# The expert stage's gather: one product for a pair of groups, in place of one for each group

## The reference, cut to what matters

```
scores = sigmoid(h @ w_router)             # 16 experts in 4 groups of 4
best   = argmax over groups of the sum of the two best biased scores
gate   = the two best experts of that group, weights normalised
a = h @ w_gate[e]; u = h @ w_up[e]         # 2048 -> 512
act = silu(a) * u * gate[e]
y  += act @ w_down[e]                      # 512 -> 2048
```

## Time and profile before

| | |
|---|---|
| median of three runs | 2128.92 us |
| span of the profiled execution, first to last instruction | 2125.9 us |
| the same execution around the span, by the median | 3.0 us |
| TensorE busy | 2011.4 us, 95% of the span, 10876 matmuls |
| VectorE busy | 1491.2 us, 70% |
| ScalarE busy | 951.2 us, 45% |
| first gather begins, first weight tile of group 0 | 1459.9 us, 1474.2 us |
| stretch 1474.2 to 2095 us: TensorE, VectorE, ScalarE busy | 610.7, 542.4, 436.4 of 620.8 us |
| bytes moved in that stretch | 318 GB/s |

### The profile page before, as it was taken

How to read it: one execution, slowest core, us unless ns; L and a number is a source line. 1 busy time by engine, 2 the same in 40 slices (tenths; PEclk the granted TensorE clock), 3 DMA queues, 4 the chain that set the end, 5 groups by cost and what they waited for, 6 DMA issues and landing times. The chain is left out here.

```text
span 2125.9 us, 27975 instructions
## 1 busy us (share of the span) xinstructions
PE 2011.4 (95%) x10876; PEld 1744.8 (82%) x10876; DVE 1491.2 (70%) x2174; ACT 951.2 (45%) x1360; POOL 7.8 (0%) x12
## 2 busy tenths in 40 slices
PE   8799999989999999999999969997999999999995
PEld 2299988977888999999999958876777887787774
DVE  0467675548877777765777733355889889889996
ACT  1333565331454322223322233343767667667773
POOL 0000000000000000000000000000000000000000
PEclk9999999999999999999999989997999999999997
DMA  9934333333433555563455566532999989899992
GB/s 374 395 123 142 118 129 110 121 125 135 158 127 134 187 208 198 200 232 118 162 209 203 199 205 230 211 123 80 330 311 357 312 312 340 307 319 338 350 348 95
DMA packets 133513, 460.96 MB, mean 217 GB/s; under 512 B 17568, under 2 KB 23520, under 8 KB 133248
## 3 DMA queue, kind: packets, MB, share of 16 engines
q1 hardware_dynamic: 133376, 459.12, 61.0%
HBM read 455.06 MB, written 4.00 MB: 216 GB/s over the span
## 5 line engine op out<-in xcount | busy, mean ns | idle before, releaser
L185 DVE TENSOR_TENSOR wlo<-raw,whi 128x1024 fp32r<-128x1024 f32 x640 | 779.4, 1223 | 426.6 <-ACT whi L179 407.1
L179 ACT ACTIVATE whi<-raw 128x1024 fp32r<-128x1024 f32 x640 | 678.8, 1061 | 839.2 <-PE bank L207 586.2
L205 PE MATMUL bank<-hhi,whi 128*128 128x384 f32 x1664 | 570.4, 343 | 9.2 <-DVE wlo L185 4.1
L206 PE MATMUL bank<-hlo,whi 128*128 128x384 f32 x1664 | 559.7, 336 | 0.0
L207 PE MATMUL bank<-hhi,wlo 128*128 128x384 f32 x1664 | 559.6, 336 | 0.0
L205 PEld LDWEIGHTS bank<-hhi,whi 128*128 128x128 f32 x1664 | 315.0, 189 | 39.5 <-issue 25.1
L206 PEld LDWEIGHTS bank<-hlo,whi 128*128 128x128 f32 x1664 | 315.1, 189 | 0.8
L207 PEld LDWEIGHTS bank<-hhi,wlo 128*128 128x128 f32 x1664 | 314.9, 189 | 0.0
L257 DVE SCALAR_TENSOR_TENSOR cond_parts<-raw,cond_padded,cond_parts 128x512 f32<-128x512 f32 x360 | 250.6, 745 | 1.3 <-DVE rstd L71 0.2
L2170 PE MATMUL bank<-whi,group_hi 128*128 128x512 f32 x512 | 204.0, 398 | 7.1 <-DVE wlo L185 5.7
L2172 PE MATMUL bank<-wlo,group_hi 128*128 128x512 f32 x512 | 201.2, 393 | 0.0
(11 more groups left out here) (323 smaller groups left out, 2015.2 us busy)
## 6 DMA issues: line engine op xcount, KB each, us to landing
raw<-in_dense SPq DMA_DIRECT2D x448, 512.0 KB, 4.5
raw<-in_moe SPq DMA_DIRECT2D x384, 512.0 KB, 5.1
merged<-in_x SPq DMA_DIRECT2D x8, 768.0 KB, 7.2
cs_rows_bc<-cs_rows SPq DMA_DIRECT2D x8, 768.0 KB, 5.0
out_y<-y_normed SPq DMA_DIRECT2D x3, 768.0 KB, 4.9
shift_rows<-cs_rows SPq DMA_DIRECT2D x2, 1024.0 KB, 11.3
pool_w_sb<-in_pool_w SPq DMA_DIRECT2D x1, 1024.0 KB, 6.9
pool_inv_count<-in_pool_inv SPq DMA_DIRECT2D x1, 768.0 KB, 4.9
```

The source lines that it names most:

```text
L179: self.nc.scalar.activation(self.whi[:, k % W, :], self.raw[:, n % R, :], ACT.Copy).then_inc(self.hi_done, 1)
L185: self.nc.vector.tensor_tensor(self.wlo[:, k % W, :], self.raw[:, n % R, :], self.whi[:, k % W, :].bitcast(F32), ALU.subtract).then_inc(se ...
L205: self.nc.tensor.matmul(out, self.whi[:, s, c], xhi[:, k, :], start=(k == 0), stop=False)
L206: self.nc.tensor.matmul(out, self.whi[:, s, c], xlo[:, k, :], start=False, stop=False)
```

## The change

The matmuls of `pick_block` keep their 256 columns, but take the matrices of both groups of a pair, 2i and 2i+1, and both halves of the result are kept. Group 0's gather ahead of the stage now brings group 1 too. In the stage there is one gather, in group 1 (i + half = 1 with half = 1), for groups 2 and 3; groups 0 and 2 have none. Since xhi and xlo now hold a pair (the same memory in all), they can be overwritten only when group 1 has done its last up tile, t=79, so PICKS has new places, t=80 to 95, in banks that gate and up have left for good. The evictions are a whole bank, 128 x 512, one per pair p, and one tile earlier than the listed number. The wait of the first tile is finer: each of the eight gate tiles u waits for the low halves it reads, but the first for all of those that lie in its bank 0 (four; ahead of group 0, seven), and up0 for all eight. The zero slots with their memset and semaphore are gone, and the tiles behind them lie elsewhere in memory. Otherwise the order of all tiles, scatters and activations is the same.

```diff
-PICKS = [(1, (24, 25), 26), (0, (27, 28), 29), (0, (31, 33), 34), (0, (36, 37), 38),
-         (1, (48, 49), 50), (7, (51, 52), 53), (7, (55, 57), 58), (7, (60, 61), 62)]
+PICKS = [(0, (80, 81), 82), (7, (83, 84), 85), (1, (85, 86), 87), (0, (87, 88), 89),
+         (7, (89, 90), 91), (1, (91, 92), 93), (7, (93, 94), 95), (1, (95, 95), 96)]
 PICK_AFTER = [max([0] + [q + 1 for q in range(p) if PICKS[q][0] == PICKS[p][0]]) for p in range(8)]
+PICK_BANK0 = max(p + 1 for p in range(8) if PICKS[p][0] == 0)
...
         pick_at = N.at
-        self.pick = sb("pick", [P, NCH, NG + 2, P], F32R)
-        place_at = N.at
+        self.pick = sb("pick", [P, NCH, NG, P], F32R)
+        place_at = N.at = pick_at + KB * (P + NE) * 4
         self.place = sb("place", [P, NG + 1, T], F32R)
...
         at = N.at = after
-        self.xhi, self.xlo = [None, None], [None, None]
-        for h in range(2):
-            self.xhi[h], self.xlo[h] = sb(f"group_hi{h}", [P, KB, P], F32R), sb(f"group_lo{h}", [P, KB, P], F32R)
+        self.xhi, self.xlo = sb("pair_hi", [P, KB, 2, P], F32R), sb("pair_lo", [P, KB, 2, P], F32R)
         self.th = sb("ff_tanh", [P, 512], F32)
...
         names = ("picked", "place_tr", "place", "weights", "weights_sb", "steps", "gathered", "group_hi", "group_lo", "tanh",
-                 "silu", "act", "act_tr", "act_hi", "act_lo", "y_hi", "y_lo", "scattered", "x_added", "gate_now", "zero",
+                 "silu", "act", "act_tr", "act_hi", "act_lo", "y_hi", "y_lo", "scattered", "x_added", "gate_now",
                  "squares", "sums", "y", "y_stored", "diagonal", "root")
...
          self.s_si, self.s_act, self.s_at, self.s_ah, self.s_al, self.s_yh, self.s_yl, self.s_sc, self.s_x,
-         self.s_gc, self.s_zero, self.s_sq, self.s_sum, self.s_y, self.s_out, self.s_diag, self.s_root) = [sem("ff_" + n) for n in names]
+         self.s_gc, self.s_sq, self.s_sum, self.s_y, self.s_out, self.s_diag, self.s_root) = [sem("ff_" + n) for n in names]
...
-    def picked(g0, i, half):
-
-        return (i * 2 + (g0 + half + 1)) * 8
+    def paired(r, i):
+
+        return (2 * r + i) * 8
+
+    def pair(x, p):
+
+        return x[:, 2 * p:2 * p + 2, :, :].rearrange("p a h s -> p (a h s)")
...
-        @block.gpsimd
-        def _(pool):
-            nc.gpsimd.memset(E.pick[:, :, NG:NG + 2, :].bitcast(F32), 0.0).then_inc(E.s_zero, 1)
-
         @block.scalar
...
                 N.tile0 = first + 2 * body * r
-                def group_high(n, p, bank, x):
+                def pair_high(n, p, bank):
                     act.wait_ge(E.s_ga, n + (p + 1))
-                    A(x[:, 2 * p:2 * p + 2, :], B[bank][:, :].rearrange("p (a b) -> p a b", a=2)[:, :, 0:P], ACT.Copy)\
-                        .then_inc(E.s_gh, 1)
+                    A(pair(E.xhi, p), B[bank][:, :], ACT.Copy).then_inc(E.s_gh, 1)
...
                         for p, (bank, _tiles, at) in enumerate(PICKS):
-                            if t == at and i * 2 + half < NG - 1:
-                                group_high(picked(g0, i, half), p, bank, E.xhi[1 - half])
+                            if t == at - 1 and i * 2 + half == 1:
+                                pair_high(paired(r, 1), p, bank)
                 for g in range(NG):
...
                 for p in range(8):
-                    group_high(g0 * 8, p, p % 2, E.xhi[0])
+                    pair_high(paired(r, 0), p, p % 2)
                 for i in range(0, 2):
...
-                def group_low(n, p, bank, x, xh):
+                def pair_low(n, p, bank):
                     dve.wait_ge(E.s_gh, n + (p + 1))
-                    V.tensor_tensor(x[:, 2 * p:2 * p + 2, :], B[bank][:, :].rearrange("p (a b) -> p a b", a=2)[:, :, 0:P],
-                                    xh[:, 2 * p:2 * p + 2, :].bitcast(F32), ALU.subtract).then_inc(E.s_gl, 1)
+                    V.tensor_tensor(pair(E.xlo, p), B[bank][:, :], pair(E.xhi, p).bitcast(F32), ALU.subtract).then_inc(E.s_gl, 1)
...
                         for p, (bank, _tiles, at) in enumerate(PICKS):
-                            if t == at and i * 2 + half < NG - 1:
-                                group_low(picked(g0, i, half), p, bank, E.xlo[1 - half], E.xhi[1 - half])
+                            if t == at - 1 and i * 2 + half == 1:
+                                pair_low(paired(r, 1), p, bank)
                 if r:
...
                 for p in range(8):
-                    group_low(g0 * 8, p, p % 2, E.xlo[0], E.xhi[0])
+                    pair_low(paired(r, 0), p, p % 2)
                 if r == 0:
...
                 N.tile0 = first + 2 * body * r
-                def pick_block(g, k, bank, bl):
+                def pick_block(i, k, bank, bl):
...
                         tok = slice(c * P, (c + 1) * P)
-                        rhs = E.pick[:, c, ds(g, 2), :].rearrange("p a s -> p (a s)")
+                        rhs = E.pick[:, c, 2 * i:2 * i + 2, :].rearrange("p a s -> p (a s)")
                         nc.tensor.matmul(o, N.hhi[:, k, tok], rhs, start=(c == 0), stop=False)
...
                 def of_group(half):
-                    return lambda k: (E.xhi[half][:, k, :], E.xlo[half][:, k, :])
+                    return lambda k: (E.xhi[:, k, half, :], E.xlo[:, k, half, :])
...
                 def group(i, half):
-                    pe.wait_ge(E.s_gl, picked(g0, i, half))
                     for t, (kind, j, u) in enumerate(FF_ORDER):
...
                         for p, (bank, tiles, _at) in enumerate(PICKS):
-                            if i * 2 + half == NG - 1:
+                            if i * 2 + half != 1:
                                 break
-                            if t == tiles[0]:
-                                pe.wait_ge(E.s_gl, picked(g0, i, half) + PICK_AFTER[p])
-                            if t in tiles:
-                                last = pick_block(i * 2 + (half + 1), 2 * p + tiles.index(t), bank, tiles.index(t))
+                            if t == tiles[0] and bank == 0 and not PICK_AFTER[p]:
+                                pe.wait_ge(E.s_act, (g0 + half) * 4 + 2 + 2)
+                            elif t == tiles[0] and not PICK_AFTER[p]:
+                                pe.wait_ge(E.s_act, (g0 + half) * 4 + 3 + 2)
+                            elif t == tiles[0]:
+                                pe.wait_ge(E.s_gl, paired(r, 1) + PICK_AFTER[p])
+                            for bl in range(2):
+                                if t == tiles[bl]:
+                                    last = pick_block(1, 2 * p + bl, bank, bl)
                             if t == tiles[1]:
                                 last.then_inc(E.s_ga, 1)
-                        if u == 0 and j > 0 and kind != "down" and i * 2 + half < NG - 1:
-                            pe.wait_ge(E.s_gl, picked(g0, i, half) + sum(at < t for _b, _t, at in PICKS))
+                        if kind == "gate" and j == 0 and half == 0:
+                            pe.wait_ge(E.s_gl, paired(r, i) + max(u + 1, PICK_BANK0 if i else 7))
+                        if kind == "up" and j == 0 and u == 0 and half == 0:
+                            pe.wait_ge(E.s_gl, paired(r, i) + 8)
                         if kind == "gate":
...
                 pe.wait_ge(E.s_pl, g0 + NG)
-                pe.wait_ge(E.s_zero, 1)
                 for p in range(8):
                     if p >= 2:
-                        pe.wait_ge(E.s_gl, g0 * 8 + p - 1)
+                        pe.wait_ge(E.s_gl, paired(r, 0) + p - 1)
                     for bl in range(2):
```

## The result

The changed kernel takes 2100.53 us in the median of four executions (2097.09 to 2104.36), against 2129.28 us for the kernel before on the same chip: ratio 0.9864, 95% interval 0.985 to 0.9878. Measured a second time, beside the experiments, it took 2100.26 us, ratio 0.9868 (0.9851 to 0.9884). It is 1.3 to 1.4% faster. The forecast was 2103.9 us with a range down to 2101; the time lies 0.5 us under that range.

A forecast was written before the change was run, and what follows sets the result against it. TensorE was taken to bound the expert stage, VectorE close behind. Terms -12.2 - 12.2 - 1.1 + 0 + 0.5 = -25.0 us took the span from 2125.9 to 2100.9 us; 3.0 us around it gave 2103.9, range 2101 to 2110.

The forecast's parts named there:

- group 0: Expert stage, group 0: its gather of the next group removed, -12.2 us, with the loads' +0.5 us counted apart.
- group 2: Expert stage, group 2: its gather removed, leaving the same work as group 3 there, -12.2 us.
- group 1: Expert stage, group 1: gather moved from t=24 to 62 to t=80 to 95, -1.1 us in sum.
- first gather: Ahead of group 0: wider evictions cost time, the finer first-tile wait saves it; sum 0, bounds -0.6 and +1.5 us.
- local stall at t=83: Group 1: the gather's first block into bank 7 waits for the activation of j=3, 0.3 us late.
- The loads' margin: Group 0's weight loads: 0.8 us between the time available and the landing, nearly used up; cost +0.5 us.
- the loads didn't bind: Rival: transfers from memory limit group 0, giving 2106 to 2110 us; chance 0.12.
- the packed gather didn't stall: Rival: evictions and hand-overs stall TensorE in group 1, first gather at its upper bound, 2106 to 2111 us; chance 0.09.
- the time wasn't hidden: Rival: TensorE isn't the bound, its removed 22 us become idle time, 2127 us; chance 0.03.
- the serial chain: Rival: in group 1's t=80 to 95 TensorE sits out each pair's whole round, 28 us, 2132 us; chance 0.03.
- group 1's t=84 to group 2's t=20 longer by about 11 us: Sign expected in the changed profile: this stretch grows by about 11 us, where group 1's gather now stands.
- group 3 unchanged within 0.3 us: Sign expected in the changed profile: group 3, which gathers nothing, keeps its time within 0.3 us.

The follow-up runs named there:

- dead2: Changed kernel with 96 gather matmuls put back into group 2, results unread and no evictions; median 2113.15 us.
- onebank: Changed kernel with seven of the eight pairs of group 1's gather in bank 1; median 2110.80 us.
- again: The changed kernel unedited, run again for a second profile; median 2100.26 us, ratio 0.9868 to the kernel before.
- before_again: The kernel before, unedited, one execution for a second profile; groups 0 to 2 took 150.51, 157.21 and 157.09 us.
- silu_early: Changed kernel with the first activation instruction on VectorE moved to three tiles behind each gate product's end; median 2092.60 us, ratio 0.9835.
- ring5: Changed kernel with five raw buffers in place of six in the whole program; median 2154.66 us.
- two_of_three: Changed kernel without the third matmul of each expert weight tile, output incomplete; one execution, span 38 us shorter.
- undo2: Changed kernel with group 2's whole old gather put back: matmuls, evictions into spare tiles and waits; median 2112.12 us.
- narrow_first: Changed kernel with the first gather's evictions 256 columns wide again, output wrong; one execution, first gather matmul to first weight tile 13.49 us.
- lastwait: Changed kernel with the first two scatters of group 3's own output at t=94 in place of t=93; median 2100.54 us.
- both2: Changed kernel with the early first activation instruction and every group's scatters of t=89 and 92 at t=88 and 90; 2095.27 us, ratio 0.9853.
- before_silu: The kernel before with only the first activation instruction moved early; 2119.63 us, ratio 0.9964.

## Why the prediction was right and wrong

Right is the mechanism, step by step, by the means of two profiles: group 0 -11.6 us (forecast -12.2, +0.5 for the loads); group 2 -12.3 (-12.2); group 1 -1.3 (-1.1); first gather -0.3 (0). The sum of these steps is -25.5 us against -25.0. Between the transposes of t=20 and t=68 the groups took 69.9 and 69.3 us (forecast 69.4), 70.8 and 70.7 (70.5), 70.3 and 70.5 (70.6). The local stall at t=83 and the lost stall at t=84 came as described. The loads' margin was used as feared, but it cost little: ScalarE waited for transfers 2.7 us in group 0, and TensorE's matmuls for low splits 1.9 us there, 0.3 more than before. None of the rivals came: the loads didn't bind, the packed gather didn't stall, the time wasn't hidden (dead2), and the serial chain, which onebank comes nearest to, costs 8.8 us when it is forced.

One sign I had worked out wrong: "group 1's t=84 to group 2's t=20 longer by about 11 us". It is longer by 8.3 us (49.5 before, 57.9 after; 49.7 and 57.8 in the second profiles). The prediction put all sixteen blocks of the gather behind the transposes of t=84. Three of them and the wait of 0.38 us lie ahead, so from t=68 to there it is 2.5 us longer (25.0 before, 27.5 after). Together they are the 11 us.

Wrong is the forecast time and with it the place of the range, in three terms outside these steps.

First, "the median of the timed runs is 2128.9, 3.0 us more than the span, which I keep". The profiled execution was not the median one. What lies around a span is 2.0 us before (in each of the eleven executions beside again 1.9 to 2.1) and 1.8 after (the changed kernel's profiled execution: 2101.34 us, span 2099.6); the rest of the 3.0 was the distance to another execution. That is 1.0 to 1.2 us too much in the forecast. To keep it meant to take the steps off 2128.9, a median of three; the later medians of the kernel before, of 9 to 12 executions, are 2126.9 to 2127.7.

Second, "group 3 unchanged within 0.3 us". It came 1.5 us shorter by the means, and this term stood at nothing in the sum. In the order of time, the profile of before shows why. TensorE, ahead of the last tiles, after its wait of 1.80 us:

```profile
2083.07 0.63 PE L2170 MATMUL bank<-whi,ff_act_hi 128*128 128x512 f32 x1
2083.50 0.63 PE L2171 MATMUL bank<-whi,ff_act_lo 128*128 128x512 f32 x1
2083.93 0.63 PE L2172 MATMUL bank<-wlo,ff_act_hi 128*128 128x512 f32 x1
```

and after the change, after a wait of 1.85 us at the same place:

```profile
2058.19 0.39 PE L2167 MATMUL bank<-whi,ff_act_hi 128*128 128x512 f32 x1
2058.42 0.40 PE L2168 MATMUL bank<-whi,ff_act_lo 128*128 128x512 f32 x1
```

The pitch is 0.43 us in the one and 0.23 in the other: the granted clock is 0.50 for that stretch of before, 1.2 GHz, and 1.00, 2.4 GHz, in the changed kernel. I had read these rows as tail and not compared their pitch. From the matmul behind the wait to the first of the last tile, the same 20 matmuls take 5.80 us in the one and 4.22 in the other, and that is nearly all of group 3's difference:

```profile
2082.02:2087.82 5.80, 5.80 (x20) 4.99 (x21) 3.72 (x8) 1.42 (x3) 0.00 (x0) 0.71 0.00 0
2057.42:2061.64 4.22, 4.22 (x20) 3.72 (x21) 3.72 (x8) 1.42 (x3) 0.00 (x0) 1.00 0.01 2
```

(5.84 in before_again, 4.22 in again.) It doesn't follow the gathers: dead2, silu_early, ring5 and two_of_three have the slow stretch too, the last three with the changed kernel's gathers as they are; again, undo2, onebank, narrow_first, lastwait and both2 don't; both profiles of before and that of before_silu do.

Third, the lower bound held the bounds of the steps but nothing for the executions themselves, which spread over 7 us.

Added up: 2103.9 less 1.2 us around the span, 0.5 in the steps and 1.5 in group 3, with 0.3 us for the later start of the first gather, gives 2101.0 us, and the two profiled executions of the changed kernel took 2101.34 and 2101.45. The medians, 2100.53 and 2100.26, lie another 0.8 to 1.2 us lower, by the scatter of the executions. As an estimate made afterwards: 2128.9 - 1.0 - 25.0 puts the middle at 2102.9; 1.5 us for group 3 and half the spread of 7 us below it, the range would start near 2098. That the time missed the stated range by 0.5 us, and not by more or not at all, is luck within this spread.

What stays open: what decides whether the slow stretch in group 3 comes, and whether it is rarer after the change or the profiles merely show it so (three of three profiles with the old gathers, four of eleven with the new).

## What to carry to other kernels

Where two stages of one loop differ by exactly the work that a change takes away, their difference, cut at instructions that can be found in both, is a good price: it was right to 0.6 us in 12. Add to a range the spread between executions, and take what lies around the span from the execution that was profiled. And a burst on the second-busiest engine, 15 waits of 0.4 us that no busy share shows, was worth about a quarter of what 192 removed matmuls were: spreading it took one moved instruction.

## What the runs showed of the hardware

The work ahead of the stage is the same in all these kernels, yet the first gather starts anywhere from 1455.3 to 1462.0 us (ring5 left out, whose ring is another). both2 and silu_early (1455.3 and 1455.55) stand at one end, before_silu at the other; silu_early and before_silu, the stretch up to the first gather:

```profile
0.00:1455.55 1455.55, 1374.24 (x7962) 1237.36 (x7963) 927.02 (x1529) 506.26 (x882) 7.08 (x11) 0.98 0.50 179
```

```profile
0.00:1462.04 1462.04, 1377.06 (x7962) 1240.51 (x7963) 929.42 (x1529) 506.11 (x882) 7.79 (x12) 0.97 0.51 178
```

The same instructions to within one, at a mean granted clock of 0.98 and 0.97. Summed over stretches of 10 us each, some 65 us of the one and 75 of the other are at 1.2 GHz, an estimate from the granted clock of each stretch; 10 us more at half the speed account for some 5 of the 6.5 us. So the short stretches at 1.2 GHz fall differently in each execution, in group 3 behind one and the same wait of 1.8 us. The whole times say the same: of the eleven executions of before beside again, the four at a granted clock of 0.978 or 0.979 took 2124.99 to 2126.85 us, the two at 0.975 took 2130.86 and 2131.53. Single executions of one kernel differ by 6.5 to 7.5 us; a difference of 1 or 2 us between two medians of four or five can't be told from that.
